# One rotary query tile for two heads, in the attention phase of a decoder block

## The chip, the cores and the metric
The kernel runs on one core of a Trainium2 chip. The metric is the time of one execution on the device, in microseconds (us). TensorE (PE) multiplies matrices, VectorE (DVE), ScalarE (ACT) and GpSimd (POOL) do the rest, and SyncE (SP) issues most DMAs. A large on-chip memory (SBUF) holds operands, a small one (PSUM) takes the results of PE.

## The reference
A decoder block for one sequence of 2048 tokens, width 1024, float32. What matters here is its latent attention:

```python
proj = h @ w_in[l]                                     # also cq, ckv (256 wide each), k_pe (64), gates
q  = (rms_norm(cq, q_norm_w)  @ w_uq ).reshape(b, s, 8, 128 + 64)
kv = (rms_norm(ckv, kv_norm_w) @ w_ukv).reshape(b, s, 8, 128 + 128)
q_nope, q_rope = q[..., :128], q[..., 128:];  k_nope, v = kv[..., :128], kv[..., 128:]
q_rope, k_rope = apply_rope(q_rope), apply_rope(k_pe)  # [x1 cos - x2 sin, x1 sin + x2 cos]
scores = (q_nope @ k_nope.T + q_rope @ k_rope.T) * 192**-0.5      # k_rope is the same for all heads
o = softmax(causal(scores)) @ v
y_b = (o * silu(b_gate)) @ w_attn_out
merged = sigmoid(g_a) * y_a + sigmoid(g_b) * y_b       # y_a: the convolution branch
out = rms_norm(x + gate * (merged @ w_out))
```

## The kernel before
Three phases follow one another. The front makes all input projections and the convolution branch, and at its end the values v of all heads, which go to DRAM. The attention phase runs the eight heads one after another. The output phase multiplies by w_attn_out, w_conv_out and w_out in units of one PSUM bank.

Every product is made from split operands: each float32 operand is kept as a high part (rounded by ACT) and a low part (the rest, subtracted by DVE or POOL), and `split3` issues three matmuls, high by high, high by low and low by high. So each operand costs an ACT instruction and then a DVE or POOL one before PE can use it.

Tokens are handled in four chunks of 512 columns. For a head, three projections per chunk make its operands: QN (the 128 rows of q_nope), QR (the rotary rows) and K (the 128 rows of k_nope). Each takes six matmuls over the 256-wide latent. The QR weights hold the 64 rotary columns and once more the same 64 with their halves swapped, so that one tile of 128 rows holds x and swapped x. DVE then rotates in three instructions (event RA: `rope_a` = x·cos, `rope_b` = swapped x·sin, their sum), ACT rounds the sum (RH) and DVE makes its low part (RL) into rows 64 to 127 of `qr`. The latents stand in two buffers `qlat`, loaded per chunk by SP.

The order on each engine comes from one list of events, made by `plan` and `with_tail`, that every engine walks. Query groups g of 512 queries are taken in the order 0, 3, 1, 2, each in four blocks of 128: S are the scores of a block, E the exponentials with their sums and, on POOL, the scaling of the probabilities (`prob`); T turns a tile of probabilities (`ps_t`, then ACT `pt_hi` and DVE `pt_lo`), and PV multiplies it by v two tiles later. The tail of a head is the stretch with the last twelve tiles; between them stand the projections of the next head. W is the split of the next head's weights (ACT, then POOL), VS that of a quarter of v (ACT, then POOL). In the last head OW and OA prepare the first unit of the output phase: a split piece of w_attn_out and the split attention output of chunk 0. A queue runs in order, so a wait holds all that stands behind it. SP's queue too is in order: per group a load of the output gate into `bg`, and the store of the finished group from the same buffer, with the loads of `qlat` for chunks 2 and 3 between them. PSUM holds five banks for scores and projections (`ps_ring`), two for turned tiles and one for the output.

The names the change touches: `load` of `ckv` and `first_weights` at the front's end (L437 to L460), the wait at L1113, `plan` and `with_tail` (L1183 to L1243), SP's `weights` and `head` (L1353 to L1420), RA at L1632 to L1639, RL at L1644, and in the output phase the first unit u = 0.

## Time and profile before
| | us |
|---|---|
| median of 3 runs | 2669.03 (2667.69 to 2669.07) |
| the profiled execution | 2673.3 |
| its span | 2671.2 |
| PE busy in it | 2579.3 (97%) |
| DVE busy | 1755.0 (66%) |
| ACT busy | 853.5 (32%) |
| POOL busy | 645.8 (24%) |
| granted TensorE clock, mean | 0.994 of full speed |

The profile is one execution recorded by the hardware, somewhat longer than the runs without it. Its span runs from the first to the last instruction. Busy is the time in which an engine executes. In a timeline row, a bracket gives the idle time before the instruction and what ended it; listed matmul durations overlap, so that what a matmul costs is the distance from one start to the next. SPq is SP's queue issuing a DMA. In time, the first head's projections begin at 1305.9 us, the first scores at 1330.1, and the output phase follows the last head.

### The profile page before, as it was taken

The numbers are of one execution on the slowest core, as the hardware profiler recorded it, in microseconds if no ns is written. First come the engines' busy times: TensorE is split into PE (matmuls) and PEld (weight loads), VectorE is DVE, ScalarE is ACT, GpSimd is POOL, SyncE is SP. The second block draws the span as 40 slices with busy tenths as digits, with TensorE's granted clock in tenths as the row PEclk, the third lists the DMA queues.
The fourth block names the chain that finished last, engine by engine and source line by source line (L and its number), as shares of the span: only waits on it lengthen the run. The fifth ranks groups of instructions, "written<-read, shape, count | busy, mean of one in ns | idle before, by whom it ended". The sixth has DMA issues, their size and how long they took to land. (4 is left out here: it accounts for less than half of the span.)

```text
span 2671.2 us, 32562 instructions
## 1 busy us (share of the span) xinstructions
PE 2579.3 (97%) x12186; PEld 2124.6 (80%) x12186; DVE 1755.0 (66%) x2069; ACT 853.5 (32%) x1691; POOL 645.8 (24%) x585
## 2 busy tenths in 40 slices
PE   5999999999999999999899999999999899999998
PEld 4777888888888888787787887887887788888887
DVE  5757977989889889575467767767767622223442
ACT  3432111111111111233255555565555520211221
POOL 2122111111111111232033133133233320323422
PEclk9999999999999999999999999999999999999999
DMA  8033312312113121379613112112112164667532
GB/s 301 9 110 106 92 52 68 87 48 88 55 57 88 48 88 48 121 260 330 205 62 107 57 67 102 61 69 100 63 65 83 60 209 158 213 207 222 191 141 79
DMA packets 193440, 305.69 MB, mean 114 GB/s; under 512 B 18137, under 2 KB 111389, under 8 KB 183356
## 3 DMA queue, kind: packets, MB, share of 16 engines
q1 hardware_dynamic: 183612, 279.12, 31.9%
q0 software_dynamic: 5120, 16.78, 1.9%
q10 hardware_dynamic: 4608, 8.39, 0.8%
q8 instruction: 70, 1.15, 0.2%
q14 instruction: 30, 0.25, 0.0%
HBM read 200.97 MB, written 103.28 MB: 114 GB/s over the span
## 5 line engine op out<-in xcount | busy, mean ns | idle before, releaser
L52 PE MATMUL ps_proj<-h_hi,w_hi 128*128 128x512 f32 x1696 | 668.8, 394 | 9.0 <-DVE h_lo L797 6.8
L53 PE MATMUL ps_proj<-h_lo,w_hi 128*128 128x512 f32 x1696 | 661.6, 390 | 0.0
L54 PE MATMUL ps_proj<-h_hi,w_lo 128*128 128x512 f32 x1696 | 661.5, 390 | 0.0
L903 DVE SCALAR_TENSOR_TENSOR acc<-u,taps_t,acc 128x2048 f32<-128x2048 f32 x240 | 628.9, 2620 | 8.5
L52 PEld LDWEIGHTS ps_proj<-h_hi,w_hi 128*128 128x128 f32 x1696 | 319.6, 188 | 77.6 <-issue 7.8
L699 POOL TENSOR_TENSOR w_lo<-raw,w_hi 128x1024 fp32r<-128x1024 f32 x53 | 178.3, 3365 | 820.9 <-ACT w_hi L491 820.9
L53 PEld LDWEIGHTS ps_proj<-h_lo,w_hi 128*128 128x128 f32 x1696 | 319.7, 188 | 66.8 <-issue 2.2
L54 PEld LDWEIGHTS ps_proj<-h_hi,w_lo 128*128 128x128 f32 x1696 | 319.4, 188 | 66.7
L1725 POOL TENSOR_SCALAR prob<-prob,rinv 128x512 f32<-128x512 f32 (+2 forms) x320 | 200.1, 644 | 351.6 <-DVE rinv L1674 351.5
L1679 DVE TENSOR_TENSOR pt_lo<-ps_t,pt_hi 128x512 fp32r<-128x512 f32 (+1 forms) x320 | 194.1, 609 | 95.9 <-ACT pt_hi L1598 92.0
L1598 ACT ACTIVATE pt_hi<-ps_t 128x512 fp32r<-128x512 f32 (+1 forms) x320 | 169.8, 533 | 235.9 <-PE ps_t L1504 235.9
L1656 DVE TENSOR_REDUCE nmax<-ps_ring 128x1 f32<-128x512 f32 (+3 forms) x288 | 174.6, 622 | 96.0 <-PE ps_ring L1489 78.0
L628 ACT ACTIVATE lat<-ps_proj 128x512 f32<-128x512 f32 x120 | 72.0, 600 | 471.8 <-PE ps_proj L54 422.7
L2011 DVE TENSOR_TENSOR o_y<-o_ps,o_g 128x512 f32<-128x512 f32 x64 | 43.9, 690 | 266.6 <-PE o_ps L54 214.9
L1590 ACT ACTIVATE prob<-ps_ring,nbias 128x512 f32<-128x512 f32 (+2 forms) x320 | 195.5, 626 | 37.5 <-DVE nbias L1662 33.1
L52 PE MATMUL o_ps<-o_a_hi,o_w_hi 128*128 128x512 f32 x512 | 200.4, 391 | 3.4 <-DVEq L2002 3.4
L53 PE MATMUL o_ps<-o_a_lo,o_w_hi 128*128 128x512 f32 x512 | 200.1, 391 | 0.0
L54 PE MATMUL o_ps<-o_a_hi,o_w_lo 128*128 128x512 f32 x512 | 200.1, 391 | 0.0
L1504 PE MATMUL ps_t<-ident,prob 128*128 128x128 f32 x1088 | 172.9, 274 | 14.8 <-POOL prob L1725 9.6
L1504 PEld LDWEIGHTS ps_t<-ident,prob 128*128 128x128 f32 x1088 | 131.1, 141 | 47.9 <-POOL prob L1725 12.3
L1519 PE MATMUL ps_o<-pt_hi,v_hi 128*128 128x512 f32 (+1 forms) x320 | 141.0, 441 | 0.7 <-DVE bg L1687 0.7
L1484 PE MATMUL ps_ring<-kn_hi,qn_hi 128*128 128x512 f32 (+2 forms) x320 | 125.3, 391 | 8.4 <-ACT prob L1590 5.0
(220 smaller groups left out, 4037.8 us busy)
## 6 DMA issues: line engine op xcount, KB each, us to landing
qlat<-qlat_dram SPq DMA_DIRECT2D x32, 1024.0 KB, 5.7
raw<-in_w_in_dram SPq DMA_DIRECT2D x52, 512.0 KB, 6.4
under_h<-in_w_ada_dram SPq DMA_DIRECT2D x8, 1024.0 KB, 10.8
ga_dram<-lat SPq DMA_DIRECT2D x8, 1024.0 KB, 5.0
gb_dram<-lat SPq DMA_DIRECT2D x8, 1024.0 KB, 5.2
agate_dram<-lat SPq DMA_DIRECT2D x8, 1024.0 KB, 5.0
conv_dram<-acc SPq DMA_DIRECT2D x8, 1024.0 KB, 3.9
v_dram<-v_st SPq DMA_DIRECT2D x4, 2048.0 KB, 8.3
```

What stands on the lines that cost most here:

```text
L52: pe.matmul(out, wh, xh, start=first, stop=False)
L53: pe.matmul(out, wh, xl, start=False, stop=False)
L54: return pe.matmul(out, wl, xh, start=False, stop=last)
L699: pool.tensor_tensor(weights(tile)[1][:], raw[tile % 2][:], weights(tile)[0][:].bitcast(F32), ALU.subtract).then_inc(lo_made, 1)
L903: dve.scalar_tensor_tensor(acc[:], u[:, n:n + S], tap(n), acc[:], ALU.mult, ALU.add).then_inc(conv_tap if n < TAPS - 1 else conv_done, 1)
L1504: mm = pe.transpose(ps_t[:, n % 2, b * P:(b + 1) * P], prob[:, x:x + P], k.ident[:])
L1519: pe.matmul(out, v_hi[:, j, :], mh, start=(j == 0), stop=False)
L1590: act.activation(prob[:, x:x + width], ps[:, chunk_no[n, c] % RING, 0:width], ACT.Exp, bias=nbias[:, n:n + 1], accum_out=rsum[:, n, c:c + ...
L1598: act.activation(pt_hi[n % SLOTS][:, s], ps_t[:, n % 2, s], ACT.Copy).then_inc(t_hi, 1)
L1656: ins = dve.tensor_reduce(to, ps[:, chunk_no[n, c] % RING, 0:width], AX.X, ALU.max, negate=True)
L1679: dve.tensor_tensor(pt_lo[n % SLOTS][:, s], ps_t[:, n % 2, s], pt_hi[n % SLOTS][:, s].bitcast(F32), ALU.subtract).then_inc(t_lo, 1)
L1725: pool.tensor_scalar(prob[:, x:x + width], prob[:, x:x + width], rinv[:, n:n + 1], 1.0, ALU.mult, ALU.mult).then_inc(normed, 1)
```

## The change
Heads are taken in pairs, four of them, with two bodies of code in the loop. The QR weights now hold the 64 rotary columns of the pair's first head and the 64 of its second; the swapped copy is gone. QR is projected once for a pair: before the first head, and in the tail of every second head. From that tile DVE rotates the first head's rows; since no swapped rows exist, `rope_b` is made in two instructions of 32 rows that read the halves crosswise. ACT copies rows 64 to 127, the second head's, scaled, into `qb` (event QB), a part of the `prob` buffer that group 0 doesn't use. SP stores `qb` to DRAM, and in the first head, before group 1, loads it back three ways: the 64 rows, and two swapped halves of 32 below them. In the tail of the first head the second head's rows are rotated from there (event RB: two products and a sum, all in SBUF), and only QN and K are projected. Around it:
- the split of v for quarters 2 and 3 stands at blocks 5 and 6 (was 6 and 7), the weight split W at block 9 (was 5), and exponentials of group 1 wait until `qb` is free;
- the front loads `ckv` in two halves of the tokens, the second one behind the first head's weights, and PE waits for each half where it needs it;
- before the first head, SP issues the latent of chunk 2 ahead of its wait for the stored values, and ACT's first QB waits for that store;
- the first output unit, 24 matmuls, runs at the end of the last head into a PSUM tile of its own, `o_first`; two pieces of w_attn_out are split in the last head and a third loaded. The output phase starts at unit 1.

The core of the diff (the rest puts head numbers in terms of pairs):

```diff
+                def load_ckv(half):
+                    s = slice(half * KHALF, (half + 1) * KHALF)
+                    for part_no, to in ((0, k.ckv_hi), (1, k.ckv_lo)):
+                        sp.dma_start(to[:, :, s].bitcast(F32), k.ckv_dram[part_no][:, :, s]).then_inc(ckv_in[half], 16)
...
-                for part_no, to in ((0, k.ckv_hi), (1, k.ckv_lo)):
-                    sp.dma_start(to[:].bitcast(F32), k.ckv_dram[part_no]).then_inc(ckv_in, 16)
+                load_ckv(0)
                 store_last((3, 4))
                 sp.wait_ge(trig_out, 16)
                 sp.wait_ge(chunk_mm, mm_no(LAST + 1, 1))
                 for to, src in first_weights(k):
                     sp.dma_start(to, src).then_inc(head_in, 16)
+                load_ckv(1)
...
-                pe.wait_ge(ckv_in, 32)
                 for m in range(2 * TT):
                     j, half = divmod(m, 2)
+                    if m % TT == 0:
+                        pe.wait_ge(ckv_in[m // TT], 32)
...
-            if s == 5:
+            if s in (5, 6):
+                ev.append(("VS", s - 3))
+            if s == 9:
                 ev.append(("W", 0))
-            if s in (6, 7):
-                ev.append(("VS", s - 4))
...
-    def with_tail(last):
+    def with_tail(a, last):
         ev, tiles, pend = plan()
...
+            ev.insert(ev.index(("E", 15)) + 1, ("OW", 1))
...
+        elif a == 0:
+            ev += [("QN", 0), ("K", 0), ("QN", 1)]
+            tiles(2)
+            ev.append(("K", 1))
+            tiles(2)
+            for c in range(NC_):
+                if 2 <= c + 2 < NC_:
+                    ev.append(("QN", c + 2))
+                ev.append(("RB", c))
+                if c < NC_ - 1:
+                    tiles(1)
+                    ev.append(("RH", c))
+                    tiles(1)
+                    ev.append(("RL", c))
+                if 2 <= c + 2 < NC_:
+                    ev.append(("K", c + 2))
+                if c == 2:
+                    ev.append(("VS", 0))
+                    tiles(2)
...
-            ev += [("QN", 0), ("QR", 0), ("RA", 0), ("K", 0), ("RH", 0), ("QN", 1), ("RL", 0)]
+            ev += [("QN", 0), ("QR", 0), ("QB", 0), ("RA", 0), ("K", 0), ("RH", 0), ("QN", 1), ("RL", 0)]
...
-                ev.append(("QR", c))
+                ev += [("QR", c), ("QB", c)]
...
-        if not last:
+        if last:
+            ev.append(("OU", 0))
+        else:
             ev += [("RH", NC_ - 1), ("RL", NC_ - 1), ("VS", 1)]
...
+        qb = prob[:, size[0] * P:size[1] * P]
...
+                def first_weights_of(q_cols, kv_cols):
 
                     sp.dma_start(raw[:, :, 0:QH], w_uq[:, :, bass.ds(q_cols, QH)]).then_inc(raw_in, 16)
-                    sp.dma_start(raw[:, :, QH:QH + HALF],
-                                 w_uq[:, :, NOPE + HALF:][:, :, bass.ds(q_cols, HALF)]).then_inc(raw_in, 16)
-                    sp.dma_start(raw[:, :, QH + HALF:QH + ROPE],
-                                 w_uq[:, :, NOPE:][:, :, bass.ds(q_cols, HALF)]).then_inc(raw_in, 16)
+                    sp.dma_start(raw[:, :, QH:2 * P],
+                                 w_uq[:, :, QH + NOPE:][:, :, bass.ds(q_cols, ROPE)]).then_inc(raw_in, 16)
                     sp.dma_start(raw[:, :, 2 * P:3 * P], w_ukv[:, :, bass.ds(kv_cols, NOPE)]).then_inc(raw_in, 16)
+
+                def second_weights_of(q_cols, kv_cols):
+
+                    sp.dma_start(raw[:, :, 0:NOPE], w_uq[:, :, bass.ds(q_cols, NOPE)]).then_inc(raw_in, 16)
+                    sp.dma_start(raw[:, :, 2 * P:3 * P], w_ukv[:, :, bass.ds(kv_cols, NOPE)]).then_inc(raw_in, 16)
+
+                def store_qb(i):
+
+                    sp.wait_ge(qb_made, (i + 2) * NC_)
+                    sp.dma_start(k.qb_dram, qb[0:ROPE, :]).then_inc(qb_out, 16)
+
+                def load_qb(i):
+
+                    sp.wait_ge(qb_out, i * 16 + 16)
+                    sp.wait_ge(t_done, At(i, 0).tile(first_tile[2] + T_CREDIT))
+                    sp.dma_start(qb[0:ROPE, :], k.qb_dram).then_inc(qb_in, 16)
+                    for half in range(2):
+                        at = ROPE + half * HALF
+                        sp.dma_start(qb[at:at + HALF, :],
+                                     k.qb_dram[HALF - half * HALF:ROPE - half * HALF, :]).then_inc(qb_in, 16)
...
-                sp.wait_ge(k.last_values_out, 16)
-                sp.sem_inc(values_stored, 1)
-                values(0, 0)
-                values(0, 1)
                 for c in (2, 3):
 
                     sp.wait_ge(proj_mm, order_of(prologue)["QR", c - 2] + 1)
                     q_chunk(c)
-
-                def head(i, last):
-                    rows = sp.snap(i * P) if not last else i * P
+                    if c == 2:
+                        sp.wait_ge(k.last_values_out, 16)
+                        sp.sem_inc(values_stored, 1)
+                        values(0, 0)
+                        values(0, 1)
+
...
+                        if g == 1 and a == 0:
+                            load_qb(i)
...
                         if n >= QB - 2 and not last:
 
-                            sp.wait_ge(proj_mm, At(i).proj(order_of(body)["QR", n - 2] + 1))
+                            sp.wait_ge(proj_mm, at.proj((order_of(second_body)["QR", n - 2] if a else order_of(first_body)["QN", n - 2]) + 1))
                             q_chunk(n)
...
+                        if n == QB - 1 and last:
+                            sp.wait_ge(next_w_lo, 1)
+                            sp.dma_start(k.o_raw[0][:], w_out[:, :, 2 * P:3 * P]).then_inc(next_piece_in, 16)
+                        store(rows, g, at.per(QB, n))
+
+                    if a and not last:
+                        sp.wait_ge(qb_in, i * 48 + 48)
+                        store_qb(i)
...
+                def first_unit(at):
+                    pe.wait_ge(exp_done, at.scores(N_CHUNK))
+                    pe.wait_ge(next_w_lo, 1)
+                    for t in range(KT):
+                        pe.wait_ge(next_a_lo, t + 1)
+                        mm = split3(pe, k.o_first[:], k.o_w_hi[0][:, t, :], k.o_w_lo[0][:, t, :],
+                                    k.o_a0_hi[:, t, :], k.o_a0_lo[:, t, :], t == 0, t == KT - 1)
+                    mm.then_inc(next_mm, 1)
...
+                        elif kind == "QB":
+
+                            m = number["QR", n]
+                            act.wait_ge(proj_mm, m + 1 if prol else at.proj(m + 1))
+                            if prol and n == 0:
+                                act.wait_ge(values_stored, 1)
+                            act.activation(qb[0:ROPE, n * TC:(n + 1) * TC], ps[ROPE:P, (N_CHUNK + m) % RING, :], ACT.Copy,
+                                           scale=SCALE).then_inc(qb_made, 1)
...
+                                if g == 1 and at.a:
+                                    act.wait_ge(rope_done, at.per(NC_, NC_))
+                                elif g == 1:
+                                    act.wait_ge(qb_out, at.pair(16, 16))
...
                             dve.scalar_tensor_tensor(a[:], bank[0:ROPE, :], SCALE, k.trig[0:ROPE, s],
                                                      ALU.mult, ALU.mult)
-                            dve.scalar_tensor_tensor(rb[:], bank[ROPE:P, :], SCALE, k.trig[ROPE:P, s],
+                            dve.scalar_tensor_tensor(rb[0:HALF, :], bank[HALF:ROPE, :], SCALE, k.trig[ROPE:ROPE + HALF, s],
+                                                     ALU.mult, ALU.mult)
+                            dve.wait_ge(qb_made, at.pair(NC_, NC_ + n + 1))
+                            dve.scalar_tensor_tensor(rb[HALF:ROPE, :], bank[0:HALF, :], SCALE, k.trig[ROPE + HALF:P, s],
                                                      ALU.mult, ALU.mult).then_inc(proj_free, 1)
                             dve.wait_ge(proj_free, m + 1 if prol else at.proj(m + 1))
                             dve.tensor_tensor(a[:], a[:], rb[:], ALU.add).then_inc(rope_sum, 1)
+                        elif kind == "RB":
+
+                            s = slice(n * TC, (n + 1) * TC)
+                            if n == 0:
+                                dve.wait_ge(qb_in, at.pair(48, 48))
+                            dve.tensor_tensor(rb[:], qb[ROPE:P, s], k.trig[ROPE:P, s], ALU.mult)
+                            dve.tensor_tensor(qb[0:ROPE, s], qb[0:ROPE, s], k.trig[0:ROPE, s], ALU.mult).then_inc(rope_step, 1)
+                            dve.wait_ge(rope_step, at.pair(NC_, n + 1))
+                            dve.tensor_tensor(qb[0:ROPE, s], qb[0:ROPE, s], rb[:], ALU.add).then_inc(rope_sum, 1)
...
+                    if u == 0:
+                        pe.sem_inc(tile_mm, 1)
+                        continue
```

DVE in the tail of a head, as its program has it (register instructions are left out here and below). First before, from the product of a group's output with its gate (`bg`) on, through the rotation of chunk 1 from PSUM (`rope_a`, `rope_b`) and the tile halves (`pt_lo`):

```order
L1679 TENSOR_TENSOR pt_lo<-ps_t,pt_hi 128x512 x2
L1687 TENSOR_TENSOR bg<-ps_o,bg 128x512
L1634 SCALAR_TENSOR_TENSOR rope_a<-ps_ring,trig 64x512
L1636 SCALAR_TENSOR_TENSOR rope_b<-ps_ring,trig 64x512
L1639 TENSOR_TENSOR rope_a<-rope_a,rope_b 64x512
L1624 TENSOR_TENSOR kn_lo<-ps_ring,kn_hi 128x512
L1679 TENSOR_TENSOR pt_lo<-ps_t,pt_hi 128x512
L1644 TENSOR_TENSOR qr<-rope_a,qr 64x512
L1679 TENSOR_TENSOR pt_lo<-ps_t,pt_hi 128x512
```

And now in the tail of a first head, from the same product on:

```order
L1808 TENSOR_TENSOR bg<-ps_o,bg 128x512
L1733 TENSOR_TENSOR kn_lo<-ps_ring,kn_hi 128x512
L1800 TENSOR_TENSOR pt_lo<-ps_t,pt_hi 128x512 x2
L1730 SCALAR_TENSOR_TENSOR qn_lo<-ps_ring,qn_hi 128x512
L1757 TENSOR_TENSOR rope_b<-prob,trig 64x512
L1758 TENSOR_TENSOR prob<-prob,trig 64x512
L1760 TENSOR_TENSOR prob<-prob,rope_b 64x512
L1800 TENSOR_TENSOR pt_lo<-ps_t,pt_hi 128x512 x2
L1765 TENSOR_TENSOR qr<-prob,qr 64x512
L1733 TENSOR_TENSOR kn_lo<-ps_ring,kn_hi 128x512
```

The rotation is still three instructions but reads `prob` (where `qb` lies) instead of `ps_ring`, and it begins with chunk 0 only after QN of chunk 2; before, it had reached chunk 1 at the gate product.

POOL in the middle of a head. Before, from the scaling of block 4 on; `head_w_l` is the weight split, `v_lo` that of v:

```order
L1725 TENSOR_SCALAR prob<-prob,rinv 128x128
L1708 TENSOR_TENSOR head_w_l<-head_raw,head_w_h 128x768
L1725 TENSOR_SCALAR prob<-prob,rinv 128x512 x3
L1725 TENSOR_SCALAR prob<-prob,rinv 128x256
L1716 TENSOR_TENSOR v_lo<-v_raw,v_hi 128x512
L1725 TENSOR_SCALAR prob<-prob,rinv 128x512 x3
L1725 TENSOR_SCALAR prob<-prob,rinv 128x384
L1716 TENSOR_TENSOR v_lo<-v_raw,v_hi 128x512
L1725 TENSOR_SCALAR prob<-prob,rinv 128x512 x4
```

Now the same stretch:

```order
L1848 TENSOR_SCALAR prob<-prob,rinv 128x128
L1839 TENSOR_TENSOR v_lo<-v_raw,v_hi 128x512
L1848 TENSOR_SCALAR prob<-prob,rinv 128x512 x3
L1848 TENSOR_SCALAR prob<-prob,rinv 128x256
L1839 TENSOR_TENSOR v_lo<-v_raw,v_hi 128x512
L1848 TENSOR_SCALAR prob<-prob,rinv 128x512 x3
L1848 TENSOR_SCALAR prob<-prob,rinv 128x384
L1848 TENSOR_SCALAR prob<-prob,rinv 128x512 x4
L1848 TENSOR_SCALAR prob<-prob,rinv 128x512
L1848 TENSOR_SCALAR prob<-prob,rinv 128x128
L1831 TENSOR_TENSOR head_w_l<-head_raw,head_w_h 128x768
```

The two v splits moved up by a block each and the weight split behind block 8; nothing stands now ahead of the four scalings after block 7.

PE at the hand-over to the output phase. Before, the last product with v, two jumps to the next phase's code, and its first matmuls into `o_ps`:

```order
L1519 MATMUL ps_o<-pt_hi,v_hi 128x128
L1520 MATMUL ps_o<-pt_hi,v_lo 128x128
L1521 MATMUL ps_o<-pt_lo,v_hi 128x128
L1348 UNCONDITIONAL_BRANCH
L1899 UNCONDITIONAL_BRANCH
L52 MATMUL o_ps<-o_a_hi,o_w_hi 128x512
L53 MATMUL o_ps<-o_a_lo,o_w_hi 128x512
L54 MATMUL o_ps<-o_a_hi,o_w_lo 128x512
```

Now, with the end of the first unit's 24 matmuls (into `o_first`) ahead of the jumps:

```order
L1601 MATMUL ps_o<-pt_hi,v_hi 128x128
L1602 MATMUL ps_o<-pt_hi,v_lo 128x128
L1603 MATMUL ps_o<-pt_lo,v_hi 128x128
L52 MATMUL o_first<-o_a_hi,o_w_hi 128x512
L54 MATMUL o_first<-o_a_hi,o_w_lo 128x512
L1390 UNCONDITIONAL_BRANCH
L2025 UNCONDITIONAL_BRANCH
L52 MATMUL o_ps<-o_a_hi,o_w_hi 128x512
```

The first unit moved ahead of the jumps; behind them stands unit 1.

## Rows read from the trace of the kernel before

**Rows 1.** The page's part 1: busy us (share of the span) x instructions
```profile
PE 2579.3 (97%) x12186; PEld 2124.6 (80%) x12186; DVE 1755.0 (66%) x2069; ACT 853.5 (32%) x1691; POOL 645.8 (24%) x585
```

**Rows 2.** Waits of TensorE: engine line waited for <- whom, us in total, times, longest
```profile
PE ps_t L1504 <- POOL prob L1725: 9.6, 9, 3.2
PE ps_ring L52 <- DMA qlat<-qlat_dram: 3.9, 1, 3.9
PE o_ps L52 <- DVEq L2002: 3.4, 1, 3.4
```

**Rows 3.** Windows: us, then busy us of PE PEld DVE ACT POOL, PEclk, DMA share, GB/s
```profile
1401.60:1431.60 30.00, 29.51 (x157) 24.38 (x156) 23.74 (x38) 14.50 (x30) 4.20 (x6) 1.00 0.30 106
1257.90:1261.90 4.00, 4.00 (x11) 3.13 (x12) 1.79 (x2) 1.65 (x3) 0.00 (x0) 0.57 1.04 349
2136.70:2141.00 4.30, 4.26 (x10) 3.42 (x11) 0.00 (x0) 1.06 (x1) 2.37 (x1) 0.50 0.66 184
```

**Rows 4.** Timeline of TensorE, tail of head 0: start, us, instruction, count, [idle <- releaser]
```profile
1405.70 0.39 PE L52 MATMUL ps_ring<-qlat,head_w_h 128*128 128x512 f32 x1
...
1407.07 0.60 PE L1504 MATMUL ps_t<-ident,prob 128*128 128x128 f32 x4
...
1415.83 0.63 PE L1504 MATMUL ps_t<-ident,prob 128*128 128x128 f32 x4 [0.49 <-DVE pt_lo L1679]
```

**Rows 5.** One tile's instructions: ns min/median/max, first and last start
```profile
L52 PE MATMUL ps_ring<-qlat,head_w_h x128: 387/389/763, 1305.9 to 2035.9; 128*128 128x512 f32 x128
```

**Rows 6.** Timeline of VectorE, tail of head 0
```profile
1411.12 0.68 DVE L1687 TENSOR_TENSOR bg<-ps_o,bg 128x512 f32<-128x512 f32 x1
1411.71 0.67 DVE L1634 SCALAR_TENSOR_TENSOR rope_a<-ps_ring,trig 64x512 f32<-64x512 f32 x1
...
1413.84 0.69 DVE L1624 TENSOR_TENSOR kn_lo<-ps_ring,kn_hi 128x512 fp32r<-128x512 f32 x1
1414.99 0.69 DVE L1679 TENSOR_TENSOR pt_lo<-ps_t,pt_hi 128x512 fp32r<-128x512 f32 x1 [0.46 <-ACT pt_hi L1598]
...
1433.26 1.75 DVE L1644 TENSOR_TENSOR qr<-rope_a,qr 64x512 fp32r<-64x512 f32 x1
```

**Rows 7.** Timeline of ScalarE, the same tail
```profile
1413.84 0.63 ACT L1569 ACTIVATE qr<-rope_a 64x512 fp32r<-64x512 f32 x1 [1.65 <-DVE rope_a L1639]
```

**Rows 8.** Timelines of GpSimd and VectorE, head 0, before the second group's tiles
```profile
1459.79 1.29 POOL L1716 TENSOR_TENSOR v_lo<-v_raw,v_hi 128x512 fp32r<-128x512 f32 x1
1461.05 3.73 POOL L1725 TENSOR_SCALAR prob<-prob,rinv 128x512 f32<-128x512 f32 x6
...
1460.08 0.16 DVE L1674 RECIPROCAL rinv<-rinv 128x1 f32<-128x1 f32 x1
```

**Rows 9.** Timelines of DVE, ACT, PE, and DMA issues, end of the front
```profile
1250.99 0.69 DVE L937 TENSOR_TENSOR u<-u,lat 128x512 f32<-128x512 f32 x1 [10.53 <-DMA sg<-agate_dram]
...
1255.46 2.00 ACT L670 ACTIVATE wv_hi<-raw 128x1024 fp32r<-128x1024 f32 x2
...
1257.88 0.47 PE L52 MATMUL ps_proj<-wv_hi,ckv_hi 128*128 128x512 f32 x1 [3.61 <-issue]
...
ckv_lo<-ckv_dram SPq DMA_DIRECT2D x1, 2048.0 KB, 18.2
```

**Rows 10.** Timelines of SP's queue and TensorE, before the first head
```profile
1312.86 0.83 SPq L1364 DMA_DIRECT2D v_raw<-v_dram  x2
...
1319.85 0.76 PE L52 MATMUL ps_ring<-qlat,head_w_h 128*128 128x512 f32 x1 [3.87 <-DMA qlat<-qlat_dram]
...
1330.10 0.33 PE L1484 MATMUL ps_ring<-kn_hi,qn_hi 128*128 128x128 f32 x1 [0.29 <-DVE rope_b L1636]
```

**Rows 11.** The page's part 6 and the timeline of SP's queue, latent chunks
```profile
qlat<-qlat_dram SPq DMA_DIRECT2D x32, 1024.0 KB, 5.7
...
1414.51 0.36 SPq L1368 DMA_DIRECT2D qlat<-qlat_dram  x1
```

More of the change, by code:

```diff
@@ L263, in front_phase @@
         wv_in = [sem(f"wv_in{i}") for i in range(2)]
-        ckv_in, head_in, next_in = sem("ckv_in"), sem("head_w_first_in"), sem("next_in")
+        ckv_in = [sem(f"ckv_in{half}") for half in range(2)]
+        head_in, next_in = sem("head_w_first_in"), sem("next_in")
         wv_hi_made, wv_lo_made, head_hi_made = sem("wv_hi_made"), sem("wv_lo_made"), sem("head_w_first_hi")
@@ L1390, in _, with reg, head @@
                     q_chunk(c)
-                def head(i, last):
-                    rows = sp.snap(i * P) if not last else i * P
+                    if c == 2:
[3 more added lines that the diff above has]
+                        values(0, 1)
+                store_qb(-1)
+                def reg(x):
+                    return x if isinstance(x, int) else sp.snap(x)
+                def head(i, a, last):
+                    at, rows = At(i, a), reg(i * (2 * P) + a * P)
                     for c in (2, 3):
-                        sp.wait_ge(v_lo_made, At(i).values(c - 2) + 1)
+                        sp.wait_ge(v_lo_made, at.values(c - 2) + 1)
                         sp.sem_inc(passed, 1)
@@ L1411, in head @@
                     for n, g in enumerate(ORDER):
-                        gate(rows, g, i * QB + n)
+                        gate(rows, g, at.per(QB, n))
+                        if g == 1 and a == 0:
+                            load_qb(i)
                         if n == 1 and last:
@@ L1421, in head @@
                             for c in (0, 1):
-                                sp.wait_ge(v_lo_made, At(i).values(c + 2) + 1)
+                                sp.wait_ge(v_lo_made, at.values(c + 2) + 1)
                                 sp.sem_inc(passed, 1)
                                 values(next_rows, c)
-                        store(rows, g, i * QB + n)
-                with sp.Fori(0, H - 1) as i:
-                    head(i, False)
-                head(H - 1, True)
+                        if n == QB - 1 and last:
[5 more added lines that the diff above has]
+                        store_qb(i)
+                with sp.Fori(0, PAIRS - 1) as i:
+                    head(i, 0, False)
+                    head(i, 1, False)
+                head(PAIRS - 1, 0, False)
+                head(PAIRS - 1, 1, True)
                 sp.wait_ge(o_out, H * QB * 16 + O_OUT_CREDIT)
                 sp.wait_ge(next_w_in, 32)
+                sp.wait_ge(next_piece_in, 16)
+                sp.wait_ge(next_mm, 1)
             @block.tensor
@@ L1631, in run @@
                             if n >= 2 or not prol:
[L1632 removed]
+                                dve.wait_ge(rope_done, at.per(NC_, NC_ + n - 1))
                             dve.wait_ge(proj_mm, m + 1 if prol else at.proj(m + 1))
@@ L1843, in _ @@
                     sp.sem_inc(v_in[i], 16)
+                sp.sem_inc(raw_in[0], 16)
                 gates(0)
                 gates(1)
-                for m in range(2, KT):
+                for m in range(3, KT):
                     piece(0, m)
@@ L1909, in _ @@
                             pe.wait_ge(lo_done, n * KT + t + 1)
-                        wh, wl = (w[:, t, :] if u < U_CONV and m == 0 else w[:, t, cols(m)]
-                                  for w in ((k.o_w0_hi, k.o_w0_lo) if u < U_CONV and m == 0 else (w_hi, w_lo)))
+                        wh, wl = (w[m][:, t, :] if u < U_CONV and m < 2 else w[:, t, cols(m)]
+                                  for w in ((k.o_w_hi, k.o_w_lo) if u < U_CONV and m < 2 else (w_hi, w_lo)))
                         mm = split3(pe, ps[:, u % BANKS, :], wh, wl,
@@ L1946, in split_hi @@
                         operand_hi(c, t, v)
-                act.sem_inc(hi_made, 1)
+                act.sem_inc(hi_made, 2)
                 act.sem_inc(hi_done, KT)
-                for m in range(1, KT):
+                for m in range(2, KT):
                     weight_hi(0, m)
@@ L1974, in weight_lo @@
                                        ALU.subtract).then_inc(lo_made, 1)
-                pool.sem_inc(lo_made, 1)
-                for m in range(1, KT):
+                pool.sem_inc(lo_made, 2)
+                for m in range(2, KT):
                     weight_lo(0, m)
```

169 lines of the change are left out of this document (96 added, 73 removed).

## The prediction

> **What bounds the kernel now.** I read the page first: TensorE (PE) is busy 97% of the span [rows 1]. Then the list of PE's waits, of which the change touches three: nine for GpSimd (POOL), 9.6 us, one for the query latent, 3.9, and one at the hand-over to the output phase, 3.4 [rows 2]; all else in attention is under 1 us at a time. So PE binds nearly everywhere, and a matmul taken out there is worth its place in the row of matmuls. What it is worth, the timeline of PE tells: a projection of six matmuls starts at 1405.70 and the next work at 1407.07 [rows 4], 1.37 us, 0.228 each (the listed 0.39 overlap). Third, the windows: in the tail of a head, where the next head is projected between the last twelve tiles, PE is busy 29.5 of 30.0 us, but VectorE (DVE) is busy 23.7 [rows 3]. That is the number on which this forecast rests: PE has only 6 us more work than DVE there, and the change takes PE work out of the tail without taking DVE work out.
>
> **Rotary tile for two heads.** Before, each head projects QN, QR and K for four chunks. The wh·latent matmuls are 128 [rows 5]: 8 heads, 4 chunks, QN and QR, 2 halves of the latent; so QR is 32 projections. Sixteen go, all in the four first tails (the tail inside the first head of a pair, which prepares the second): 4 x 1.37 = 5.5 us of PE in each, 21.9 in all. What takes their place? The rotation of a first tail (RB) is three DVE instructions on SBUF, as RA was, plus RL. An instruction of that size takes one place of 0.7 us in DVE's queue: RA's first instruction starts at 1411.71 and K's after it at 1413.84, three in 2.13 [rows 6]. So DVE has the same count.
>
> I walk DVE's queue with t from the first QN of the tail (1401.58; the window's start). QN0, K0, QN1, two tiles, K1, two tiles keep PE busy to t = 9.4 and give DVE only 6 us, so it idles, and the four RBs come in the second half. QN2's low part starts at 11.6 (matmuls to 10.7, ScalarE (ACT) 0.6, and the next slot). From there to the low part of the last tile DVE has 24 instructions (2 QN, 2 K, 9 of RB, 3 RL, 8 tiles) at 0.60 to 0.72 (a slot, start to start), the three narrow tiles 0.7 less together: 15.4. Three times a tile waits because ACT splits RH first, which hangs on RB: RH runs from 1413.84, 0.63, the tile's high part behind it, and DVE goes on at 1414.99 after an idle 0.46 [rows 6, 7]; 1.15 after the sum, of which QN or K fills 0.6: 3 x 0.57 = 1.7. The latent for QN3 stands in SP's queue behind the store of the last group's output and the gate load. Before, its issue at 1414.51 [rows 11] came 3.4 after DVE began the product with the gate, 1411.12 [rows 6]; now that product begins about t = 6.9 (three projections, two tiles), the issue is at 10.3 and the data are there 5.7 later [rows 11], at 16.0, against a PE ready at 14.4. Of these 1.6, DVE has other work for 1.05: 0.55. Then RB3, the gate product and RL3, 3.5. Sum 11.6+15.4+1.7+0.55+3.5 = 32.8. Before, RL3 ends at 1435.01 [rows 6], t = 33.4. PE, with its matmuls alone at 24, waits some 5 us for tile halves and starts the next head at 29.6, not 30.0. The first scores then wait for DVE and the exponentials, so 0.5 a tail is won; the 5.5 become waits. One hole, before the tile after K3, is some 3 us, and after holes of that size the granted clock fell to 0.57 and 0.50, that is to 1.2 GHz for part of it [rows 3], about 1.7 us at the smaller; part falls where PE waits anyway, so I book 0.6. First tails: +0.1 each, +0.5 in all. Ends: -5.5 (all matmuls show) and +1.7, so -21.9 to +6.8 over four. I take the walk since DVE's rows leave no way round.
>
> RL3 took 1.75 us where others take 0.69 [rows 6], at 1433.26, when POOL splits v as it does in every tail. The Trainium skill (SBUF — State Buffer, "Who interferes with whom") says that a DVE instruction with two SBUF inputs contends with a GpSimd instruction that reads SBUF; the trace agrees. By that rule the change is exposed, 12 more such instructions a first tail in place of 4; but POOL is busy only 4.2 of the 30 us [rows 3], before RB0 and beside RL2, so by rule and row alike I add nothing; one hit a tail would be 1.06 x 4 = 4.2.
>
> **Second tails** (three of them): the QR tile now holds both heads' 64 rows, so the swap of halves is two DVE instructions of 32 rows, not one of 64: width sets the time, so +0.7 per chunk, and ACT copies the other head's rows, +0.6 per chunk in an ACT busy 14.5 of 30 us [rows 3], hidden. The first +0.7 falls into DVE's waits for ACT. The second lands on the wait already there, PE at 1415.83 for a tile half [rows 4]: +0.8. The third has 0.3 of slack: +0.45. The fourth stands before S0 and S1: +0.75. 2.0 x 3 = +6.0; ends 0 and 2.8 x 3 = 8.4.
>
> **POOL's order.** In each head a tile of the second group waited 0.8 us for prob: POOL splits v at 1459.79 and reaches the probabilities only at 1461.05, though their reciprocal was ready at 1460.24 [rows 8]. With the v splits at blocks 5 and 6 and the weights at 9, POOL starts about 0.2 after the reciprocal: 0.6 x 8 = -4.8. Ends 0 and, with all of the nine waits but the one of 3.2 at the end gone [rows 2], -6.4. The weight split moves behind block 8, 15 us before anything needs it.
>
> **Front.** PE stopped for 3.6 us at 1254.3 to 1257.88. The queue behind it: DVE waited 10.5 us, to 1250.99, for a gate piece; ACT needs DVE's sum before its last drains of PE, and it splits wv only behind them, from 1255.46; the low part and PE follow at 1257.88 [rows 9]. The piece shares the DMA with 4 MB of ckv, whose second part took 18.2 us [rows 9]. With 2 MB fewer ahead of it, at the 349 GB/s of that stretch [rows 3], it lands 6.0 us sooner. The seventh of the last eight tiles stands before the split; PE ends it 24 matmuls before 1254.3, at 1248.8. So wv is split from 1249.5, its first half ready by 1252, and the half of ckv that PE needs is in: no stop. -3.7, and -1.7 for the 4 us at clock 0.57 behind it [rows 3]: -5.4. Ends 0 and -5.4.
>
> **Before the first head.** The stop of 3.9 us for the latent, at 1319.85 [rows 10], goes: its load stood behind the values (1312.86 [rows 10]); now it goes out after twelve matmuls from 1305.9 [rows 5], at about 1310.6, and is in at 1316.3, when PE comes to it. But DVE now waits for ACT's copy, which may not write before the values are stored, 1312.9, so to 1313.5; from there seven slots a chunk (RA 4, K, RL, QN) for three chunks, 15.1: RA3's last product ends at 1328.6, so S0 starts at 1328.7, not 1330.10 [rows 10]: -1.4, less 0.7 for a clock that may fall in the hole of 3.6 us before it: -0.7. Ends -5.5 and +1.7.
>
> **Hand-over.** The stop of 3.4 us [rows 2] and the slow first 5.6 us (0.50, [rows 3], 2.7 lost): one unit of 24 matmuls, 5.5 us, moves into it. The store that the stop waited for lands under it; left is the barrier, some 1.6. So 3.4 - 1.6 = 1.8 less of the stop, and half of the 2.7, 1.4: -3.3 with rounding. Ends 0 and -6.1.
>
> At nothing: the store and load of qb on SP (before RB0 by 12 us), the other order of SP's loads, the second out-weight split (POOL and ACT idle there), the new waits before block 8 (30 us after their stores), the 2-fold code.
>
> Sum: +0.5 +6.0 -4.8 -5.4 -0.7 -3.3 = -7.7. Against the profiled execution's 2673.3 us (span 2671.2) that is 2665.6; the median of the runs lies 4.3 below it, at 2669.03: **2661.3 us**.
>
> **Rivals.**
> - PE's matmuls do show (13%): DVE catches up earlier than I walk, the first tails give 21.9 less 3 of waits. For it: 97% [rows 1]; against: 23.7 busy of 30 [rows 3]. 2661.3 - 19.4 = 2642.
> - The clock follows the holes (15%, the slow side): PE, emptied, stops over 3 us in four first tails and once before the first head, and the fall comes late, over the scores behind, 2.7 each as at the hand-over [rows 3] instead of my 0.6 and 0.7. 5 x 2.7 - 3.1 = +10.4, and the hand-over's half (+1.4): 11.8 on top of -7.7, +4.1: 2673. From 1.9 each on the change is slower. For it: both rows show it after a stop of 3.4 to 3.7; against: work trickles in these holes.
> - The front stop stays (15%): the gate piece is late for its own reason; +5.4: 2666.7.
> - qb comes late (7%): 2 MB took 18.2 us in a full queue [rows 9], so this 1 MB some 9.1 from t = 0.5; past 11.6 each us counts four times. At half as long again, 14.1, +9.8: 2671. Against it: the latent's 1 MB needs 5.7 [rows 11].
> The Trainium skill (SBUF — State Buffer, "Door 1") says that 64 partitions reach only half the DMA ports, 196 GB/s: by that an estimate of 5 to 6 us for the 1 MB, and with its start some 7, still in time. No row here has such a load in a quiet queue.
>
> **How the numbers follow.** Forecast 50% (own range 2656 to 2668). This kernel's measurement tells 0.2%, 5.3 us, from no change; so faster is below 2663.7: 0.37 of the forecast, the first rival, a little of the third: 0.52. Within 0.2%: 0.31. Slower: the clock's most and a tail of others, 0.17. Range: 2647 (halfway into the first rival) to 2673.
>
> **What would show it.** Right: PE's single waits for tile halves (DVE pt_lo) grow to some 15 to 20 us, four times over in the first tails; DVE busy 95% and more from RB0 on there; head pairs some 1 to 2 us longer or equal; the wait for prob 0.2, not 0.8; no stop before the values, and the first scores 1 to 2 us nearer to the first projection than the 24.2 (1305.9 to 1330.1) of before. Wrong: first tails of 25 us, or a clock under 0.9 in the scores after them, or DVE waiting at RB0 for a DMA.

## The result, and the profile after

The changed kernel takes 2697.36 us (median of 4 runs, 2687.55 to 2699.49) against 2669.05 before: a ratio of 1.0093, 95% interval 1.0078 to 1.0107. By the ratio it is slower by some 25 us, between the two medians by 28; 2661.3, faster, was forecast. The profiled execution took 2699.49, its span is 2697.7.

The page's first line and the list of PE's waits, in the columns of [rows 1, 2]:

```profile
PE 2577.6 (96%) x12090; PEld 2118.3 (79%) x12090; DVE 1759.4 (65%) x2085; ACT 856.2 (32%) x1703; POOL 646.6 (24%) x585
```

```profile
PE ps_t L1586 <- DVE pt_lo L1800: 20.0, 15, 2.9
PE ps_ring L52 <- DMA qlat<-qlat_dram: 19.4, 9, 4.3
...
PE ps_t L1586 <- POOL prob L1848: 4.8, 9, 3.2
...
PE o_ps L52 <- PEq L1390: 0.7, 1, 0.7
```

96 matmuls are gone from PE's count (16 QR projections of six), yet PE is busy as long as before: 2577.6 for 2579.3. Part of the reason is the clock: where the granted clock is half, the same matmul is listed with 0.63 us for 0.39, and the starts lie 0.43 apart for 0.23. The waits the change aimed at have gone (POOL's from 9.6 to 4.8, the hand-over's from 3.4 to 0.7, the one of 3.6 in the front), but the latent's rose from 3.9 to 19.4 and those for tile halves from 5.2 to 20.0.

From PE's timeline I took the length of each stretch: a tail is measured here from the next head's first QN matmul to its first scores. A first tail is one inside the first head of a pair, a second tail one inside the second head. All in us:

```
stretch                          before           after                     change   forecast
front, to the first QN           1305.9           1300.1                     -5.9     -5.4
first QN to first scores           24.2             22.8                     -1.4     -0.7
first tails (4)                  30.1 each        34.8, 36.0, 37.4, 35.9    +23.8     +0.5
second tails (3)                 30.1 each        33.8, 33.8, 32.1           +9.5     +6.0
rest of the seven heads          71.5 each        73.1 to 70.8               +3.4     -4.2
last head's scores to the end     630.0            627.1                     -2.9     -3.9
sum                                                                         +26.5     -7.7
```

Of the forecast for POOL, -4.2 belong to the seven heads and -0.6 to the last line, which holds the last head and the hand-over. The matmuls at a slow pace behind a tail fall into the rest of the heads, which is why that line is up and not down. The other lines of the surroundings came near to their forecast, and the loss is in and behind the tails.

The first tail of the first pair, on PE, SP and DVE (timelines as in [rows 4, 6, 10]). Below, a number behind an event is its chunk: QN3 is QN of chunk 3, and t counts from the first QN of the tail.

```profile
1414.49 0.53 PE L52 MATMUL ps_ring<-qlat,head_w_h 128*128 128x512 f32 x1 [2.55 <-DMA qlat<-qlat_dram]
1414.83 0.63 PE L53 MATMUL ps_ring<-qlat,head_w_h 128*128 128x512 f32 x1
1415.25 0.63 PE L54 MATMUL ps_ring<-qlat,head_w_l 128*128 128x512 f32 x1
...
1426.75 0.44 PE L1586 MATMUL ps_t<-ident,prob 128*128 128x128 f32 x2 [2.92 <-DVE pt_lo L1800]
...
1430.06 0.39 PE L1601 MATMUL ps_o<-pt_hi,v_hi 128*128 128x256 f32 x1 [1.44 <-DVE pt_lo L1800]
```

```profile
1395.63 0.48 SPq L1416 DMA_DIRECT2D prob<-qb_dram  x1
1396.15 1.04 SPq L1419 DMA_DIRECT2D prob<-qb_dram  x2
1397.55 0.34 SPq L1428 DMA_DIRECT2D qlat<-qlat_dram  x1
1398.18 1.04 SPq L1424 DMA_DIRECT2D v_raw<-v_dram  x2
1403.47 0.36 SPq L1437 DMA_DIRECT2D attn_dram<-bg  x1
...
1408.69 0.33 SPq L1433 DMA_DIRECT2D bg<-bgate_dram  x1
1409.13 0.36 SPq L1428 DMA_DIRECT2D qlat<-qlat_dram  x1
```

```profile
1408.97 0.69 DVE L1730 SCALAR_TENSOR_TENSOR qn_lo<-ps_ring,qn_hi 128x512 fp32r<-128x512 f32 x1 [2.71 <-ACT qn_hi L1652]
...
1427.75 1.80 DVE L1765 TENSOR_TENSOR qr<-prob,qr 64x512 fp32r<-64x512 f32 x1
```

And the same store and gate load before the change, in the tail of head 0:

```profile
1411.82 0.36 SPq L1377 DMA_DIRECT2D attn_dram<-bg  x1
1414.07 0.33 SPq L1373 DMA_DIRECT2D bg<-bgate_dram  x1
```

The tail begins at 1395.97. The reader is to see three things. PE waits for the latent of chunk 3 until t = 18.5 (16.0 was forecast): SP's store of the finished group, issued at 1403.47, lets the gate load go only at 1408.69, 5.2 us later (2.3 before), and the latent stands behind it. Then PE waits twice for tile halves (`pt_lo`), which DVE makes. And DVE, which idled 2.71 us early on, is the one that is late in the second half.

The clock, in the windows' columns [rows 3]: right behind that latent, and at the first scores after the first tail of the third pair:

```profile
1414.50:1418.20 3.70, 3.70 (x11) 2.98 (x12) 0.97 (x2) 0.75 (x2) 0.00 (x0) 0.54 0.00 0
1859.00:1864.00 5.00, 5.00 (x22) 4.50 (x22) 3.47 (x8) 2.17 (x6) 1.64 (x2) 0.50 0.37 118
```

0.50 is 1.2 GHz for all of the window. Added up over PE's timeline, matmuls at a slow pace behind the stops of the four first tails come to some 18 us, behind those of the second tails 2, behind the one before the first head 2.7. Some of the 18 lie inside the tails, where PE would partly have waited for DVE in any case.

### The profile page after: what moved, and what is told of

The parts are those of the page before. It is cut to its first block and busy times, and to the rows that moved or that the text cites. A ratio compares the mean times of both kernels' runs of the same rounds, so it can differ in the third digit from the quotient of the medians.

```text
span 2697.7 us, 32117 instructions
## 1 busy us (share of the span) xinstructions
PE 2577.6 (96%) x12090; PEld 2118.3 (79%) x12090; DVE 1759.4 (65%) x2085; ACT 856.2 (32%) x1703; POOL 646.6 (24%) x585
```

## The experiments

Tails by run, in order (first, second, first, ...; without pairs simply seven tails), from PE's timeline:

```
before          30.1 in each of seven
changed         34.8 33.8 36.0 33.8 37.4 32.1 35.9
latent_early    32.7 34.0 32.3 33.9 31.9 32.1 31.3
qb_unloaded     31.6 34.4 31.2 33.8 31.3 32.1 32.3
rb_one          34.5 34.0 32.2 34.1 31.8 32.1 30.8
k_repeated      37.0 34.4 35.9 34.2 36.0 32.1 34.4
swap_one        32.6 32.8 32.3 32.5 32.5 30.3 30.8
rb_early        30.9 33.9 31.2 34.4 32.1 32.1 30.4
rb_early_pool   29.8 33.9 29.3 34.1 29.3 32.1 27.8
pairs_unrolled  27.0 32.2 28.7 32.2 27.8 32.2 27.9
rest_alone      30.1 in each of seven
two_a_turn      30.1 32.2 30.1 32.3 30.1 30.1 30.1
qr_short        28.3 in each of seven
rest_unrolled   30.1 to 30.2 in each of seven
```

**The latent asked for in time** (latent_early):

```diff
-                        if n >= QB - 2 and not last:
+                        if n >= QB - 2 and not last and a:
...
+                        if n == QB - 2 and not a:
+                            for c in (2, 3):
+                                sp.wait_ge(proj_mm, at.proj(order_of(first_body)["QN", c - 2] + 1))
+                                q_chunk(c)
```

> In the first heads of the pairs SP asks for the latent of chunk 3 right behind that of chunk 2, ahead of its wait for the gate buffer; else as the changed kernel (2697.4). Theory (late latent): in the first tails PE stops 2.5 to 4.3 us for that latent, 13.8 us in four, and the granted clock falls behind it. The load lands at the time of chunk 2's, so these four stops go, and with them the slow matmuls right behind (1.3 to 1.6 each): 2697 - 13.8 - 5.5 = about 2678, the clock behind the next hole (2.9 us, before the tile after K3) perhaps staying. Rival (VectorE binds the first tails): VectorE is then the next to be late, its work from QN2 to the end of the tail is the same, only 3 of the 13.8 come back: 2694.

2679.39 us, ratio to before 1.0038 (1.0026 to 1.0049): 18 us of the 28 between the medians came back (15 of 25 by the ratios), as the late-latent theory had it. The four stops for chunk 3 are gone; behind them DVE shows:

```profile
1413.33 0.63 PE L1590 MATMUL ps_t<-ident,prob 128*128 128x128 f32 x4 [1.61 <-DVE pt_lo L1804]
...
1418.68 0.44 PE L1590 MATMUL ps_t<-ident,prob 128*128 128x128 f32 x2 [2.92 <-DVE pt_lo L1804]
```

A new wait of 1.61 after K2, and the 2.92 after K3 to the hundredth as before: the rival named the right next limit.

**No rows loaded back** (qb_unloaded; 16 of 2048 columns in each of the three loads):

> The 1 MB of second-head rotary rows is not loaded back in the first heads: 16 of 2048 columns only, so the second heads rotate stale rows; all else as the changed kernel. Theory (the burst of DMAs at the start of the first tails delays the gate buffer's store and both latents): from the store's issue to the gate load 2.3 us as before, not 5.2; QN2's wait of 1.05 gone, QN3's down from 2.5-4.3 to about 1: 2697 - 3 - 10 = about 2684. Rival (the latent waits for its own place in SP's queue, not for bandwidth): the lag of 5.2 and QN3's wait stay within 0.5 us, time 2694 to 2697.

2679.19 us, 1.0030 (1.0016 to 1.0044). SP's queue there:

```profile
1398.57 0.36 SPq L1437 DMA_DIRECT2D attn_dram<-bg  x1
1401.19 0.33 SPq L1433 DMA_DIRECT2D bg<-bgate_dram  x1
```

2.6 us from store to gate load for 5.2. With the 1 MB of rows on top of 1 MB of latent and 0.5 MB of values, all asked for in one go, a 256 KB store on which SP's queue hangs is held up. QN2's wait is gone and QN3's is down to 1.1, 1.2, 1.4 and, in the last, 2.3: 6.0 for 13.8 in all. So the rows are more than half of that stop; the rest is the latent's place in SP's queue, of which the prediction had counted 1.6 a tail.

**One instruction for the rotation** (rb_one: two of RB's three instructions left out):

> The rotation of the second heads' rows is one VectorE instruction a chunk in place of three (one product; the second product and the sum are left out): 8 fewer in each first tail, 5.7 us of VectorE each. Late-latent theory: QN3's stop of 2.5 to 4.3 stays, the hole before the tile after K3 (2.9) and the one of 1.4 behind it go, with the clock that falls after them: 2697 - 4 x 4.3 - some 8 = about 2672. VectorE-bound rival: the tails shrink by all of VectorE's 5.7 and the clock stays up: 4 x 5.7 + 18 = 41 less, 2656.

2677.67 us, 1.0027 (1.0014 to 1.0039), above both and nearer to the first. QN3's stops stayed at 4.2, 3.0, 2.4 and 2.5; the 2.9 after K3 fell to 0.45. The 1.44 beside the split of v stayed, which I had counted as gone. So there are two causes, the late latent and DVE's chain, worth 18 and 20 us between the medians when taken away alone, each with the slow matmuls behind its stops; no run takes away both whole, so the two need not add up.

**PE made to work more** (k_repeated):

```diff
+                        for again in range(3 if not prol and at.a == 0 and c >= 2 else 1):
```

> The changed kernel (2697.4), with PE made to do more: in the first tails the projections K of chunks 2 and 3 are issued three times over into the same bank, the last one counting. 24 more matmuls a first tail, 5.5 us, just ahead of the two holes (latent of chunk 3, tile after K3), 21.9 us in all: as much as the change took out. Theory (PE only waits there, and the clock follows the holes): the repeats fall into the holes, the tails get no longer, and the clock stays up behind them: 2697 - 0 to 12, about 2690. Rival (PE's work still counts): 2697 + 10 to 22.

2692.93 us (2690.36 to 2698.55), 1.0078 (1.0061 to 1.0095), against 1.0093 (1.0078 to 1.0107) of the changed kernel: 22 us of matmuls put back, and no time lost. They stand just ahead of the holes and not where QR stood, but they show that in these tails as much PE work as the change took out fits into PE's waits. The half about the clock was not borne out: holes of 2.0 us remained (14.8 us for tile halves in all), and the mean clock was 0.983, no higher than 0.986.

**The swap in one instruction** (swap_one, on top of latent_early; the halves aren't swapped):

> On top of the early latent (2679.4): in prologue and second tails VectorE makes rope_b in one instruction of 64 rows as before; the halves are then not swapped, that part of the rotation is left out. Theory (the second tails' +3.7, +3.7 and +2.0 are the fourth instruction's 0.7 a chunk and the half clock that follows): second tails back to 31 us or less, before the first head 1 to 2 us less: 2679.4 - 9 - 2 = about 2668. Rival (ScalarE's copy QB and the larger loop do it): second tails keep 32 to 33, total 2674 to 2677.

2675.76 us (2671.45 to 2685.24), 1.0022 (1.0008 to 1.0036), in the rival's range. The second tails went from 34.0, 33.9, 32.1 to 32.8, 32.5, 30.3. The third, behind the loop, is then that of before, with ScalarE's copy still in it: the fourth instruction cost 1.2 to 1.8 us a tail, and the copy nothing. The first two keep 2.2 to 2.5 more, so something sits at the jump back: of the rival's two causes, the copy is out and the larger loop is left.

**The rotation of chunk 0 earlier** (rb_early: `("RB", 0)` ahead of `("QN", 2)`, on top of latent_early):

> On top of the early latent (2679.4): in the first tails the rotation of chunk 0 stands ahead of QN of chunk 2, in a stretch where VectorE idles 2.8 us with the rows already landed. Theory (in the first tails VectorE's order binds: it idles early and is late in the second half): the wait of 1.8 us before the tile after K2 goes, the one of 3.1 us after K3 shrinks by what is left; 4 x 2.5 plus 4 us of clock: about 2666. Rival (the late end is set by the chain sum, ScalarE's split, tile half, each time afresh): only the 1.8 goes: 2672 to 2675.

2676.77 us, 1.0021 (1.0011 to 1.0031): 2.6 less than latent_early, a little above the rival's range and 11 above the theory. The wait after K2 went from 1.61 to 0.58, and that after K3 stayed 2.93. It is not a backlog carried through the tail but a chain made afresh: three instructions of RB in front of a tile's low part.

**The swapped product on GpSimd** (rb_early_pool, on top of that):

```diff
+                        elif kind == "RB":
...
+                            pool.tensor_tensor((ra[0], ra[1], rb, ra[0])[n][:], qb[ROPE:P, s], k.trig[ROPE:P, s],
+                                               ALU.mult).then_inc(swap_step, 1)
```

> As the run with chunk 0's rotation early, and GpSimd makes the product of the swapped rows for all four chunks, which takes 4 x 0.7 us off VectorE in each first tail. Theory (VectorE's amount of work binds): another 4 x 2.5 and the clock of the last hole: about 2654, the first tails at 28 us or less. Rival (GpSimd and VectorE, both reading two operands in SBUF, hold each other up as in the rows where RL takes 1.8 us beside a split of v): one or two hits of 1.1 a tail, 2660 to 2666.

2666.87 us (2660.57 to 2670.47), 0.9980 (0.9970 to 0.9991): the upper end of the rival's 2660 to 2666, not the theory's 2654. First tails of 27.8 to 29.8, and 10 us less; the wait after K3 fell from 2.93 to 2.10. Rows of POOL and of DVE in the first tail:

```profile
1401.52 2.64 POOL L1852 TENSOR_TENSOR rope_a<-prob,trig 64x512 f32<-64x512 f32 x2 [2.56 <-DMA prob<-qb_dram]
1404.24 1.26 POOL L1852 TENSOR_TENSOR rope_b<-prob,trig 64x512 f32<-64x512 f32 x1
```

```profile
1404.57 1.47 DVE L1765 TENSOR_TENSOR prob<-prob,trig 64x512 f32<-64x512 f32 x1
...
1420.94 1.80 DVE L1774 TENSOR_TENSOR qr<-prob,qr 64x512 fp32r<-64x512 f32 x1
```

DVE's 0.69 becomes 1.47 while GpSimd multiplies. There is only one such hit at the front of the tail, since GpSimd is done before DVE needs SBUF twice again; the 1.80 beside the split of v is the old one.

**The change without the pairs** (rest_alone: the kernel before with only the orders and loads around the pairs):

> The kernel before with all that the change does around the pairs and none of the pairs: v splits at blocks 5 and 6 and weight split at 9, ckv in halves, chunk 2's latent ahead of the values before the first head, first output unit in the last head. By the changed kernel's trace the front gave 5.9 and the hand-over 2.9; POOL's order should give 8 x 0.6 = 4.8 and the latent before the first head 3.9, as no copy for a second head stands in the way: 2669 - 17.5 = about 2651.5. If these gains live from the pairs, or the clock takes them back, it comes out above 2660.

2654.42 us (2653.20 to 2655.44), 0.9944 (0.9928 to 0.9961). It beats both kernels: 15 us of gain, all outside the pairs, which cost some 40 on top of it (1.0093 against 0.9944; 43 between the medians). Of the expected 17.5 it lacks 2.5; before the first head PE still stops 1.7 there, now for DVE.

**Two heads a turn** (two_a_turn, on top of rest_alone):

```diff
-                with pe.Fori(0, H - 1) as i:
-                    run(body, At(i))
+                with pe.Fori(0, H // 2 - 1) as i:
+                    run(body, At(i * 2))
+                    run(body, At(i * 2 + 1))
+                run(body, At(H - 2))
```

> The run without pairs (2654.4) with its loop over heads turned half as often: two copies of the same body a turn, the last two heads behind the loop, the same work in the same order. In the changed kernel the tails at a jump back of the longer loop took 33.8 us, the one without 32.1, VectorE idle 2.7 to 2.9 us behind the jump for nothing the profile shows; before, it went on at once. Theory (a jump back in the longer loop costs some 2 us): three of the seven tails 2 us longer and slow matmuls behind them: 2654.4 + 6 to 11 = about 2662. Rival (the fourth rotary instruction alone moved the edge there): 2654 to 2655, all tails 30.1.

2657.46 us (2656.50 to 2660.55), 0.9955 (0.9939 to 0.9972). The same work in the same order, and exactly the two tails with a jump back (a loop of three turns has two) take 32.2 and 32.3 for 30.1; I had counted three. The whole grew by 3.0 us only, less than the forecast 6 to 11 and less than the two stops with their half pace (some 7.7): in the profiled executions the stretch before the first head was 2.3 shorter (19.4 for 21.7), which this edit doesn't explain. The jump's 2 us are read from the tails, not from the total. PE at the first scores there, with the idle time that nothing in the profile explains, and the half pace behind it (1.8 us each):

```profile
1521.25 0.32 PE L1507 MATMUL ps_ring<-kn_hi,qn_hi 128*128 128x128 f32 x1 [1.97 <-issue]
```

**Fewer QR matmuls and nothing else** (qr_short, on top of rest_alone; five of six matmuls of each QR in the tails are left out):

> The run without pairs (2654.4), where in the tails of the seven heads each QR projection is one matmul in place of six (five are left out): 20 x 0.227 = 4.5 us less of PE in each tail, nothing else changed, no second head's rows, no more instructions on any engine. Theory (VectorE's list of work binds the tail): the tails shrink from 30.1 to no less than 29, 2654.4 - 0 to 7, about 2650, and stops of over 2 us may bring the clock down. Rival (PE's matmuls count when nothing else is put in): 7 x 4.5 = 31.5 less, 2623.

2641.47 us (2638.70 to 2644.29), 0.9895 (0.9879 to 0.9912): 13 less than rest_alone, where its theory had 0 to 7 and its rival 31.5. The first tail of each, windows, first rest_alone and then qr_short:

```profile
1390.80:1420.80 30.00, 29.48 (x157) 24.33 (x155) 23.62 (x38) 14.42 (x31) 4.28 (x6) 1.00 0.29 106
```

```profile
1387.70:1416.00 28.30, 25.77 (x138) 20.37 (x136) 23.68 (x38) 14.44 (x30) 4.17 (x6) 1.00 0.31 112
```

4.5 us of PE taken out of each tail shorten it by 1.8, even with no second head's rows, no burst and no new instruction. The bound of 29 that the theory set was too high. In the second window PE is idle 2.5 of 28.3 us, in four stops that all end with DVE; DVE itself is idle 4.6, so what holds PE up is the order in which DVE gets to its work, not a full DVE.

**The pairs without a loop** (pairs_unrolled: rb_early_pool, with the loop written out) and **the same for the kernel without pairs** (rest_unrolled):

> The pairs with early latent, early rotation of chunk 0 and the swapped product on GpSimd (2666.9), with the loop over pairs written out: no jump back. Theory of the jump: second tails 32.1 for 33.9 to 34.1, twice or three times, and the half clock behind them gone: 2666.9 - 4 to 9 = about 2660. Rival (fetching new code costs as much as jumping): no change, 2666.

> The run without pairs (2654.4) with the loop over heads written out. In its trace the jump back costs nothing at PE, but ScalarE loads a table of 1.28 us at the head of each turn, ahead of the first exponentials; without the jump that may go. If it binds the first scores: 7 x 0.5 less, 2651. If it is hidden, or new code costs as much: 2654.

2655.02 us (2653.19 to 2658.77), 0.9940 (0.9924 to 0.9957), and 2654.85 us (2651.59 to 2655.91), 0.9938 (0.9921 to 0.9954). The pairs take 12 us less than with the loop, more than the forecast 4 to 9, and all their second tails are 32.2. The second tails give only 3.5 us of it; the first tails, where no jump back stands, are 4.8 shorter too, which no run explains. Without pairs nothing changes. So the pairs at their best (first tails 27.0 to 28.7, second 32.2) come out level with no pairs at all.

## Why the prediction was wrong

- **The step that failed is the walk of the first tails**, "+0.1 each, +0.5 in all": it measured +23.8. Its structure was right (DVE, not PE, sets the tail; k_repeated, rb_one and qr_short show it), and so was its hole of "some 3 us" after K3 (2.92 in each of the four), but the walk summed a DVE that is never starved and a DMA queue that is quiet. It had RL3 done at t = 32.8; it was 37.8. The misses: QN2's low part at t = 13.0, not 11.6, as the latent of chunk 2 came 1.05 late; QN3's latent at 18.5 to 20.2, not 16.0, in the first three as the store took 5.2 and not the 2.3 of before (3.8 in the fourth); and RL2 took 1.80 beside the split of v, a hit that the forecast left at nothing. PE's stops for that latent were 13.8 us in the four tails.
- The 5.7 us for a latent [rows 11] and the 3.4 from the product to its issue were read in a queue without the 1 MB that the change itself puts there. I asked of the new load only whether it comes in time itself (it does, DVE never waited for it), and not whom it delays. qb_unloaded shows that to be the cause of most of it (stops of 6.0 in place of 13.8).
- **The clock** was booked at 0.6 a first tail. The slow matmuls come to 3.3 to 5.5 a tail, of which an unmeasured part hides in PE's waits. The rival "the clock follows the holes" had the right sign, the places and about the size (2.7 each behind the tail), with a chance of 15%; it lacked the second fall, behind the latent's stop, and took the latent's stops as the walk had them. Exactly what brings the clock down is told by no run: it was half behind these stops, but k_repeated, with PE better filled, kept the same mean.
- **Second tails**, +6.0: measured +9.5, near to three times 2.0 and two jumps back of 1.7. The fourth instruction was right in size (1.2 to 1.8 us for 2.0 a tail); "the 2-fold code" at nothing was wrong: each jump back cost 2.1 us and slow matmuls behind (in two_a_turn).
- **POOL's order**: right. Its wait fell from 9.6 to 4.8, and without pairs the rest of a head is 70.9 for 71.5. In the changed kernel the slow first scores ate it: the rest of the seven heads is 3.4 longer, not 4.2 shorter.
- **Front**: right, and by its steps. The gate piece came 6.0 sooner than in [rows 9], ACT split wv at 1249.45 (1249.5 was forecast), and the stop is gone:

```profile
1244.99 0.69 DVE L944 TENSOR_TENSOR u<-u,lat 128x512 f32<-128x512 f32 x1 [3.67 <-DMA sg<-agate_dram]
...
1249.45 2.01 ACT L677 ACTIVATE wv_hi<-raw 128x1024 fp32r<-128x1024 f32 x2
```

- **Before the first head**: the -1.4 is exact, but for another reason in part: the latent still cost 1.9 and 0.7, and the hole before the scores was 3.0, with 2.7 us lost to slow matmuls behind it, where 0.7 was booked.
- **Hand-over**: of the -2.9 of its line 0.6 are POOL's, so -2.3 for -3.3; the stop went from 3.4 to 0.7.
- **The signs** that the prediction named for itself came mixed: PE's waits for tile halves did grow to 20.0 and the wait for prob did fall to 0.2, but DVE was not busy 95% from RB0 on (79% in the first tail, with one idle time of 2.73 before QN3's low part), and the clock in the scores behind the tails was under 0.9, which was named as a sign of being wrong.

## What to carry to other kernels

Where one engine is busy 97% of the whole and another 79% of one stretch, price the stretch: there, work taken off the first is worth only what the second's order lets through (here 1.8 of 4.5 us in qr_short; in the pairs' best form the first tails win 1.4 to 3.1 of 5.5, and the second tails, at +2.1, take most of it back). Price a load that is added to a stretch by what stands behind it and beside it in the queues, above all by small stores whose completion a queue waits for, and not by its own deadline. When a change comes as a bundle, run its parts apart: the surroundings alone were worth 15 us, and the idea in the middle cost some 40.

## What the runs showed of the hardware

- A jump back in a loop whose turn holds two heads' code idled PE 1.97 and 2.03 us, one whose turn holds one head's code did not: tails of 32.2 and 32.3 for 30.1, with the same instructions. Where between the two lengths it begins, and what the engines wait for, no run shows. DVE behind such a jump in the changed kernel, the idle time ended by nothing the profile knows:

```profile
1754.15 0.62 DVE L1777 TENSOR_REDUCE nbias<-ps_ring 128x1 f32<-128x128 f32 x2 [2.87 <-issue]
```

- A store of 256 KB, issued 4 to 8 us behind 2.5 MB of loads, kept its queue waiting 5.2 us, against 2.3 before the change and 2.6 with 1 MB of the loads left out.
- Two operands in SBUF on DVE and on GpSimd at the same time: the DVE instruction of 0.69 us took 1.47 beside a product (rb_early_pool), 1.80 beside a split of v. The Trainium skill (SBUF — State Buffer, "Who interferes with whom") says so of a GpSimd instruction that reads SBUF; the trace agrees.
